# Expert rows of a two-layer encoder: gathered in half rows, spread over both sweeps, and held by a count of tiles

## What is computed

```python
def chunk(xc):                                  # xc: 128 positions x 2048
    q = (xc @ w_query).reshape(PEER_CHUNK, PEER_HEADS, 2, PEER_HALF)
    sc = jnp.einsum('chpd,hpkd->chpk', q, sub_keys, preferred_element_type=jnp.float32)
    s1, i1 = lax.top_k(sc[:, :, 0], PEER_TOPK)
    s2, i2 = lax.top_k(sc[:, :, 1], PEER_TOPK)
    cand_s = (s1[..., :, None] + s2[..., None, :]).reshape(PEER_CHUNK, PEER_HEADS, kk2)
    cand_i = (i1[..., :, None] * PEER_N_KEYS + i2[..., None, :]).reshape(PEER_CHUNK, PEER_HEADS, kk2)
    top_s, pos = lax.top_k(cand_s, PEER_TOPK)
    idx = jnp.take_along_axis(cand_i, pos, axis=-1)
    gate = jax.nn.softmax(top_s, axis=-1)
    u = jnp.take(expert_u, idx, axis=0)
    act = jax.nn.gelu(jnp.einsum('chkd,cd->chk', u, xc, preferred_element_type=jnp.float32),
                      approximate=False)
    vsel = jnp.take(expert_v, idx, axis=0)
    return jnp.einsum('chk,chkd->cd', (gate * act).astype(xc.dtype), vsel)
```

## Time and profile before

| | us |
|---|---|
| median of three runs | 4158.66 |
| lowest, highest | 4155.15, 4164.67 |
| the profiled execution | 4165.31 |
| its span, first to last instruction | 4163.5 |
| PE busy | 3808.6 (91%) |
| DVE busy | 2260.3 (54%) |
| POOL busy | 676.0 (16%) |
| ACT busy | 429.4 (10%) |
| DMA | 1077.41 MB, mean 259 GB/s |

### The profile page before, as it was taken

How to read it: one execution, slowest core, us unless ns; L and a number is a source line. 1 busy time by engine, 2 the same in 40 slices (tenths; PEclk the granted TensorE clock), 3 DMA queues, 4 the chain that set the end, 5 groups by cost and what they waited for, 6 DMA issues and landing times. The chain is left out here.

```text
span 4163.5 us, 63554 instructions
## 1 busy us (share of the span) xinstructions
PE 3808.6 (91%) x26660; PEld 3414.8 (82%) x26660; DVE 2260.3 (54%) x3941; ACT 429.4 (10%) x1020; POOL 676.0 (16%) x664
## 2 busy tenths in 40 slices
PE   6997889999999999999869978899999999999998
PEld 5776774888999888898857867748889998888987
DVE  3975751893387444324249657518924864443242
ACT  1013210100111000000010222101001100000000
POOL 5510000021011211111055100000210111111110
PEclk9998899999999999999979989999999999999999
DMA  4330015499799999979644300145997999999896
GB/s 150 115 128 9 1 42 156 160 387 374 268 383 384 390 421 421 418 296 421 255 123 131 112 9 1 62 137 188 378 374 276 382 390 394 421 421 403 306 421 243
DMA packets 279470, 1077.41 MB, mean 259 GB/s; under 512 B 46052, under 2 KB 144728, under 8 KB 163992
## 3 DMA queue, kind: packets, MB, share of 16 engines
q1 hardware_dynamic: 223896, 670.72, 43.1%
q0 software_dynamic: 55296, 402.68, 23.8%
HBM read 1071.23 MB, written 2.10 MB: 258 GB/s over the span
## 5 line engine op out<-in xcount | busy, mean ns | idle before, releaser
L1742 PE MATMUL bank<-ex_W,ex_tile 128*128 128x160 f32 x8192 | 1165.2, 301 | 85.6 <-DMA ex_tile<-in_peer_v 84.8
L1742 PEld LDWEIGHTS bank<-ex_W,ex_tile 128*128 128x128 f32 x8192 | 1118.0, 190 | 136.2 <-DMA ex_tile<-in_peer_v 128.3
L1669 PE MATMUL bank<-ycT,ex_tile 128*128 128x160 f32 x8192 | 1155.0, 301 | 51.8 <-DMA ex_tile<-in_peer_uT 51.7
L1669 PEld LDWEIGHTS bank<-ycT,ex_tile 128*128 128x128 f32 x8192 | 1122.7, 191 | 76.3 <-DMA ex_tile<-in_peer_uT 71.8
L1936 DVE SCALAR_TENSOR_TENSOR ex_sums<-ex_row,ex_weight,ex_sums 128x2048 f32<-128x2048 f32 x186 | 436.9, 2349 | 326.7 <-DMA ex_row<-in_peer_v,ex_rows 326.7
L1930 DVE CUSTOM_DVE_ANT_0 ex_row<-ex_row,ex_h_wide 128x2048 f32<-128x2048 f32 x192 | 437.4, 2289 | 232.4 <-DMA ex_row<-in_peer_u,ex_rows 230.5
L1627 POOL DMA_INDIRECT ex_row<-in_peer_u,ex_rows x192 | 222.5, 1159 | 2098.3 <-DVE ex_rows L1900 1184.3
L358 PE MATMUL pj_bank<-pj_hT,pj_piece 128*128 128x256 f32 x2048 | 465.3, 387 | 15.4 <-DVE s_CT L724 8.7
L358 PEld LDWEIGHTS pj_bank<-pj_hT,pj_piece 128*128 128x128 f32 x2048 | 392.5, 194 | 83.4 <-issue 13.1
L1627 POOL DMA_INDIRECT ex_row<-in_peer_v,ex_rows x192 | 188.5, 982 | 1028.2 <-DVE ex_sums L1936 694.6
L824 PE MATMUL bank<-arena,ycT 128*128 128x512 f32 x512 | 222.4, 593 | 2.0 <-PEq L909 2.0
(11 more groups left out here) (376 smaller groups left out, 3152.2 us busy)
## 6 DMA issues: line engine op xcount, KB each, us to landing
ex_tile<-in_peer_uT SPq DMA_DIRECT2D x256, 1024.0 KB
ex_tile<-in_peer_v SPq DMA_DIRECT2D x256, 1024.0 KB
pj_piece<-in_w_in SPq DMA_DIRECT2D x32, 2048.0 KB, 8.9
arena<-in_w_out SPq DMA_DIRECT2D x16, 2048.0 KB, 8.1
query_w<-in_peer_w_query SPq DMA_DIRECT2D x16, 1024.0 KB, 5.9
ex_row<-in_peer_u,ex_rows POOLq DMA_INDIRECT x192
ex_row<-in_peer_v,ex_rows POOLq DMA_INDIRECT x192
x<-in_x SPq DMA_DIRECT2D x1, 2048.0 KB, 8.9
```

Source lines behind the costliest of these rows:

```text
L1669: mm = mmul(o, ring[:, j % SLOTS, k * P:k * P + P], hT[k // 4][:, k % 4, 0:DENSE], start=(k == 0), stop=(k == KT - 1))
L1742: mm = mmul(bank[:, at_, lo:lo + DENSE], ring[:, i % SLOTS, m * P:m * P + P], W[:, j, :], start=(j == 0 and m % 3 == 0), stop=(j == TILES ...
```

## The change

Each row is fetched by two indirect DMAs of 4 KB per partition instead of one of 8 KB. The tables are viewed as twice as many rows of 1024 numbers; `rows` holds for each step the number of the first half, 2 x (expert + layer's base), and of the second, one more. `rows_of` writes both (24 instead of 12 small operations, and one more for `half_on`). A row's semaphore rises by 32 instead of 16. The rows are dealt out anew: 40 instead of 30 before tile 64, then 31 in 40 tiles instead of 9 in 10, so that 89 instead of 87 are served by the end of the first sweep. The exponentials of the first block move on ACT from tile 60 to tile 30, `weigh(0)` from behind tile 66 to behind tile 54, `share(0)` on DVE from behind row 29 to behind row 31, the widening of set 1 from tile 90 to 76 and that of set 2 from tile 36 to 24 of the second sweep. POOL waits from row 93 on also for PE's count of tiles: row n is not issued before tile 6/5 x (n - 93) of the second sweep is done.

```diff
-BEFORE = 30
-WIDEN_0, EXPS_1, WIDEN_1, FOLD_0 = 2, 16, 90, 114
-WIDEN_2, FOLD_1, FOLD_1_AT = 36, 80, 152
+BEFORE = 40
+WIDEN_0, EXPS_1, EXPS_0, WEIGH_0, WIDEN_1, FOLD_0 = 2, 16, 30, 54, 76, 114
+WIDEN_2, FOLD_1, FOLD_1_AT = 24, 80, 152
...
 def served(j):
 
-    return BEFORE + max(j - FIRST + 1, 0) * 9 // 10
+    return BEFORE + max(j - FIRST + 1, 0) * 31 // 40
+
+
+def second_sweep_pace(n):
+
+
+    ahead = n - served(TILES - 1) - RING
+    return TILES + ahead * 6 // 5 if ahead >= 0 else 0
...
-        rows = sb(st, "ex_rows", [P, SETS, STEPS], U32)
+        rows = sb(st, "ex_rows", [P, SETS, 2, STEPS], U32)
+        half_on = sb(st, "ex_half_on", [P, 1])
...
-        tables = [t[n].rearrange("l e d -> (l e) d") for n in ("peer_u", "peer_v")]
+        tables = [t[n].rearrange("l e (h d) -> (l e h) d", h=2) for n in ("peer_u", "peer_v")]
...
-                pool.wait_ge(rows_ready, SETS * 4)
+                pool.wait_ge(rows_ready, SETS * 4 * 2)
                 for n in range(ROWS_IN):
                     s, table, step = n // (2 * STEPS), n // STEPS % 2, n % STEPS
                     if n >= RING:
                         pool.wait_ge(place_free, n - RING + 1)
-                    nc.gpsimd.indirect_dma_start(
-                        out=place[:, n % RING, :], out_offset=None, in_=tables[table][:, :],
-                        in_offset=bass.IndirectOffsetOnAxis(ap=rows[:, s, step:step + 1], axis=0))\
-                        .then_inc(row_in[n % RING], 16)
+                    if second_sweep_pace(n):
+                        pool.wait_ge(tile_mm, second_sweep_pace(n))
+                    for half in range(2):
+                        nc.gpsimd.indirect_dma_start(
+                            out=place[:, n % RING, half * D // 2:(half + 1) * D // 2], out_offset=None,
+                            in_=tables[table][:, :],
+                            in_offset=bass.IndirectOffsetOnAxis(ap=rows[:, s, half, step:step + 1], axis=0))\
+                            .then_inc(row_in[n % RING], 16)
...
-                    if j == FIRST - 4:
+                    if j == EXPS_0:
                         exps(0)
...
-                    if served(j - 1) < STEPS <= served(j):
+                    if j == WEIGH_0:
                         weigh(0)
...
                 def rows_of():
+                    do(V.tensor_scalar(half_on[:], layer_base[:], 0.5, None, ALU.add), wait=False)
...
-                            V.tensor_scalar(rows[quarter(q), s, :], flat[own(s), STEPS * q:STEPS * q + STEPS],
-                                            layer_base[own(s), :], None, ALU.add).then_inc(rows_ready, 1)
+                            for half, base in enumerate((layer_base, half_on)):
+                                V.tensor_scalar(rows[quarter(q), s, half, :], flat[own(s), STEPS * q:STEPS * q + STEPS],
+                                                base[own(s), :], 2.0, ALU.add, ALU.mult).then_inc(rows_ready, 1)
...
-                    dve.wait_ge(row_in[n % RING], layer * (16 * ROWS_IN // RING) + 16 * (n // RING + 1))
+                    dve.wait_ge(row_in[n % RING], layer * (32 * ROWS_IN // RING) + 32 * (n // RING + 1))
...
-                for n in range(2 * PEER_H, served(FIRST - 1)):
+                for n in range(2 * PEER_H, STEPS):
                     serve(n)
                 share(0)
+                for n in range(STEPS, served(FIRST - 1)):
+                    serve(n)
```

## The result

The changed kernel takes **4046.28 us** (median of 4 runs, 4045.36 to 4051.23) where the kernel before, run beside it, takes 4157.61: a ratio of 0.9734, 95% interval 0.972 to 0.9749. That is 111 us less; 3989 was forecast, in a range of 3956 to 4090. The profiled execution took 4051.2 with a span of 4049.4.

What follows compares the result with a forecast made beforehand. TensorE, kept waiting for tile loads by rows on full DMA engines, bounds the kernel; gains of 27 + 57 and 29 + 57, 170 us, off 4158.7 give 3989, range 3956 to 4090 (main case to 4045).

Steps and rivals of the forecast that it cites:

- The ceiling and the floors: TensorE's lost time, 208 us in both layers, caps any gain; unstarved it needs 4.37 a tile, 565 for sweep two.
- Half rows shift the share: DMA queues take turns by packet, 4 KB against 8 KB: tiles can have two thirds, 281 GB/s, 3.74 us each.
- Rival one: DMA queues share by bytes, so only the dealing out acts: sweep two gains 36 us a layer; 4087, chance 0.15.
- TensorE stops waiting: Tile loads at 3.74 us, below 4.37, no longer hold TensorE; sweep two takes 575, a gain of 57 us.
- Sweep one: Loses 9 us: 3 at the start, 3 at tile 30, 3 from tile 104; gains 27 and 29 us.
- The stall at tile 30: ACT waits there for the best scores, stalling TensorE 3 us; a wait of ACT above 5 us would show error.
- The price of a row: On the DMA engines twice as many packets raise a row from 2.49 to 2.60 us, at most 2.72.
- Rows 5.8 us apart: Rows get the remaining 181 GB/s, one in 5.8 us, which covers POOL's 2.5 to 4.3 us a row.
- The hold: In sweep two 1.2 tiles a row, 5.24 us, is tighter than the DMA engines can follow; binds only at first.
- The deal: Ten more rows before tile 64, where VectorE waited 80.1 us, cost TensorE nothing if tiles come first.
- rival three: POOL's issues each wait out a VectorE operation, 7.1 us a row: 4269, chance 0.03; decides from 6.6 a row.
- Rival two: A transfer's fixed share puts 3.9 us between a row's halves on the DMA queue, 6.4 a row: 4127, chance 0.04.

Runs made afterwards that it cites:

- the last run: The changed kernel with 97 rows in sweep one and no hold, given four tile slots and three row places instead of three and four: 4007.80 us.
- the second run: The kernel before with half rows alone, each row in two transfers of 4 KB a partition, no new deal, no hold: 4035.10 us, ratio 0.9714.

## Why the prediction was right, and where its size was off

The sign and the range hold, and of the cause the first half: the bandwidth shifts to the tiles. That TensorE then stops waiting does not hold, and 57 of the 170 us forecast did not come. By the prediction's own steps:

- **The ceiling and the floors.** 4.37 a tile, 565 for sweep two: the last run reached 577.9 and 578.6 with a stall at the folds of set 1 of 12.2 and 13.4 us in them; without it that is 565 to 566, though no run shows it. Right as far as is known.
- **Half rows shift the share** (turns by packet). Right in kind: half rows alone bring 120 us, whole rows with the same deal 16, and with four slots tiles take 241 GB/s while rows of 4 KB packets take the rest. The page of the Trainium skill that the prediction named, "DMA: Bandwidth & Descriptors", section "Queues, rings and completion order", gives turns by packet; with 8 KB on both sides the bytes were even the earlier trace rows, with 4 KB against 8 KB they leaned to the tiles, so the traces agree in direction. Whether it is the size of the pieces that counts or their number is not shown: the run with 64 partitions and the one with half tiles were to tell, and neither does. Rival one (turns by bytes) would have left tiles at 4.97: it falls with the second run. Its price, 4087, was too low besides: whole rows with the new deal and the hold, which is what that rival comes to, took 4139.03, outside of the range given, since the hold did not keep tiles at 4.56. A full share of two to one was never seen, since TensorE can't use more than 240.
- **"TensorE stops waiting": the step that failed.** It was reasoned in rates, 281 GB/s offered against 240 used. But a slot comes free when its tile is done and is needed again two tiles later, 8.74 us, and a load lands in a median of 8.2 to 8.3 us, with a spread from 7.9 to 9.5: of the 54 loads from 3500 to 3750, 16 took more than 8.74. So about every fourth tile comes late. Why the landing varies was not looked into. Priced: 0.25 us x about 120 tiles is some 30 us in a sweep two, where 10 were forecast lost and 28 were measured (593.4 against 565); both layers, 37 of the missing 57. The four-slot run shows it: the same landing of tiles, no waits for loads. The prediction had named this sign itself ("if TensorE still waits for tiles beside gathers"), and it came. The total stayed in the range because what is left of the wait costs 0.25 us a tile, where it cost 0.60 before.
- **Sweep one** was to lose 9 and lost 19 (622 against 603), the other 20. The stall at tile 30 was forecast at 3; it was 5.41 and 4.91 (ACT's wait there, a sign of error from 5 us on, was 15), and its removal is worth 6.6 to 7.2 a layer, so some 4 of the 10 us over are its. The best scores came at 2961.3 only, while TensorE was ready at about 2958.8. The rest are mostly waits for loads, 14.9 us in both layers. The hold on the rows there didn't shorten them, but it hardly shortened the row queue either; with four slots they are gone. So they too belong to the step above.
- **The price of a row** was put at 2.60 us (bounds 2.49 to 2.72): 414 to 415 GB/s at full engines make 2.53 for a transfer of either kind. With tiles at 2.49 as forecast, a row's part is an estimated 2.58: 250 us less 54.0 tiles at 2.49, over 44.8 rows, from the queues from 3500 to 3750. Right.
- **Rows 5.8 us apart:** measured 5.74 (14 rows in 80.33 us from 3701.04). Right, and with room: nothing waited for the rows at the end.
- **The hold** was said to bind only at first. It ended 31.6 us of POOL's waiting, and without it the time is the same. Right. What it could do was missed: at 1.4 tiles a row it brings 18 us with three slots.
- **The deal** was to let sweep one take ten more rows for nothing and remove the stop at tile 80. The stop shrank from 77.5 to 19.65 us, but not by the deal: with half rows and the old deal it is 2.4 us. And it was worth nothing, since rows didn't set the end of sweep two: with the stall at tile 30 mended the deal is worth 0 (4035.56 against 4035.10).
- **POOL** (rival three) was judged right for two issues a row, at most one of them stretched. The mechanism is real, as the quarter rows show: four issues, one stretched to 2.0 to 3.0 us, some 6.7 us a row, beyond the 6.6 from which the rival was to decide. That the 4255.53 lie near its price of 4269 is chance: that was worked out for two issues that each wait out an operation, 7.1 us a row.
- **Rival two** (3.9 us between a row's halves): rows at 5.74 with full engines exclude it. The rule of the Trainium skill named there ("DMA: Bandwidth & Descriptors", section "Anatomy of one DMA") gives about 2.0 us beside the bytes for each transfer. By the traces that does not add up over halves in flight together; how much of a tile's 8.2 us to landing is such a fixed part, no run here shows.

Open: the share that turns alone give between two queues that are never empty and have pieces of different size. In every run here either TensorE's need, the ring or the hold bounded one side.

## What to carry to other kernels

Compare not only rates but times: a load's landing beside the time for which its slot is free. Where these are within some per cent of each other, another slot (23 us here), or a competing queue that is kept short (18 us), brings what is left after the share of bandwidth has been bettered; where a ring of the other stream has a place to spare, trade it. Smaller pieces on the queue that can wait help the one that can't, until the engine that issues them becomes the bound: two pieces gained 120 us, four were 99 us slower than whole rows, and cutting the stream that is waited for lost the gain too.

## What the hardware showed that was not expected

- **Gathers of 64 partitions, 8 KB each.** Two of them for one of 128 made full engines move 246 GB/s instead of 421, for the tiles as well (landing 18.7 us), and the kernel 29% slower, with the same bytes and only the completion packets more. The trace shows packets that take longer (q0: 30.0% of 16 engines' span of 5371.9 us for 49152 large packets, 525 ns each, where 23.8% of 4163.5 made 322). Why wasn't found. The Trainium skill, "DMA: Bandwidth & Descriptors", section "Rules for kernel authors", advises against two transfers to disjoint halves of the partitions because they serialize on the same engines; that names no loss of rate, and here it was two fifths.
- **The price of packets.** With rows always waiting in the queue, full engines moved 421 GB/s with 8 KB packets and 414 to 415 with rows of 4 KB. 394 were moved both with tiles and rows of 4 KB and with rows of 2 KB, but there the row queue was short (gathers landed in 9.0 and 7.4 us). A short row queue alone did nearly as much: 397 GB/s at a share of 1.00, with 8 KB tiles and 4 KB rows under the hold of 1.4 tiles. So the 394 are not shown to be the price of packets, and a share of 1.00 does not mean one rate.
- **An issue beside VectorE.** A gather's issue takes 0.94 us alone and up to 3.0 beside a row operation of VectorE. With quarter rows it falls on one issue of each row, in every row.
